# A spatial gating block whose second half is projected with tokens on partitions, and its norm taken along the free axis on VectorE

## The reference

```
z = gelu(x @ w_in_odd)                  # 288 x 1024 times 1024 x 2048
u, v = z[:, :1024], z[:, 1024:]
v = layer_norm(v, sgu_ln_g, sgu_ln_b)   # over the 1024 channels of a token
mix[t, g, c] = sum_s w_s[g, t, s] * v[s, g, c] + b_s[g, t]
                                        # 8 groups g of 128 channels; s <= t in chunks of
                                        # 128 tokens; in each sample over its own 4 tokens
out = (u * mix) @ w_out_odd
x = layer_norm(ALPHA * x + out, ln_g, ln_b)
```

## Time and profile before

| | |
|---|---|
| time, median of 3 runs | 1298.22 us (1296.71 to 1301.53) |
| the profiled execution: time | 1299.01 us |
| its span | 1297.3 us |
| mean granted TensorE clock | 0.952 |
| busy: TensorE | 1195.8 us (92%) |
| busy: VectorE | 493.1 us (38%) |
| busy: ScalarE | 264.3 us (20%) |
| busy: GpSimd | 143.1 us (11%) |
| DMA | 359.97 MB, 277 GB/s over the span |
| the gating block | from about 749 us to about 849 us |

### The profile page before, as it was taken

The page is one execution under the profiler, slowest core; times in us unless marked ns, Lnnn a source line. Parts: engine busy times, 40 slices in busy tenths (PEclk is TensorE's granted clock), DMA queues, the critical chain, the costliest instruction groups (busy, mean ns, idle before and its releaser), DMA issues.

```text
span 1297.3 us, 27118 instructions
## 1 busy us (share of the span) xinstructions
PE 1195.8 (92%) x10881; PEld 780.1 (60%) x10882; DVE 493.1 (38%) x1297; ACT 264.3 (20%) x553; POOL 143.1 (11%) x236
## 2 busy tenths in 40 slices
PE   9999877899997989999998899899998989999996
PEld 7677655566774765555554577676775744555543
DVE  0014561924152362333333500524242553343357
ACT  0013642121141040111111211302230311111113
POOL 2001897000000000000000200000000000000020
PEclk9999889899998979999998999789999889999999
DMA  9746678963378488998999943213367689999994
GB/s 327 260 137 186 206 220 298 389 235 130 130 260 322 146 330 332 383 428 367 429 424 411 382 173 130 69 65 130 130 226 294 228 358 425 427 364 407 417 376 149
DMA packets 89052, 359.97 MB, mean 277 GB/s; under 512 B 7063, under 2 KB 7079, under 8 KB 72586
## 3 DMA queue, kind: packets, MB, share of 16 engines
q1 hardware_dynamic: 81042, 333.73, 67.4%
q0 software_dynamic: 7792, 24.93, 5.3%
q10 hardware_dynamic: 144, 0.27, 0.1%
HBM read 341.48 MB, written 17.85 MB: 277 GB/s over the span
## 4 chain that ended last, share of the span: by engine, by line
PE 69%; DMA 12%; DVE 11%; issue 4%; ACT 3%; SPq 1%; DVEq 0%; POOLq 0%; POOL 0%; ACTq 0%
PE acc L793 37%; PE psS L793 15%; DMA by_slot<-arena 9%; PE psV L793 5%; DVE acts L1603 3%; PE psN L793 2%; PE acc L1142 2%; DVE arena L2015 2%; DMA ring<-in_w_exp_up 2%; PE acc L923 1%; PE psN L1243 1%; PE acc L1273 1%; DMA arena<-by_slot,arena 1%; ACT arena L1482 1%; DMA arena<-in_mem_prompt 1%
## 5 line engine op out<-in xcount | busy, mean ns | idle before, releaser
L793 PE MATMUL acc<-acts,ring 128*128 128x288 f32 x1280 | 319.2, 413 | 3.4 <-DVE acts L1893 1.5
L793 PEld LDWEIGHTS acc<-acts,ring 128*128 128x128 f32 x1280 | 247.1, 193 | 74.5 <-issue 2.5
L793 PE MATMUL psS<-arena,acts 128*32 128x256 f32 (+1 forms) x2864 | 224.2, 390 | 3.0 <-issue 1.7
L793 PEld LDWEIGHTS psS<-arena,acts 128*32 128x32 f32 (+1 forms) x2864 | 98.5, 110 | 82.7 <-issue 42.8
L2015 DVE COPY arena<-psV 32x256 f32<-32x256 f32 x192 | 80.6, 420 | 176.0 <-DMA by_slot<-arena 164.2
L1482 ACT ACTIVATE arena<-acc 128x1024 f32<-128x1024 f32 (+6 forms) x86 | 67.5, 810 | 110.3 <-PE acc L793 35.2
L793 PE MATMUL psS<-ring,acts 128*32 128x256 f32 x1344 | 81.9, 394 | 6.9 <-DMA ring<-in_w_exp_up 3.3
L793 PE MATMUL psS<-acts 128*32 128x256 f32 x672 | 79.4, 386 | 1.6 <-issue 1.6
L2535 POOL DMA_DIRECT2D by_slot<-arena x48 | 23.6, 491 | 447.9 <-DVE arena L2015 447.9
L793 PEld LDWEIGHTS psS<-ring,acts 128*32 128x32 f32 x1344 | 43.9, 113 | 43.3 <-issue 16.3
L2379 ACT ACTIVATE acts<-psS 128x256 f32<-128x256 f32 x54 | 20.7, 383 | 219.8 <-PE psS L793 216.1
(11 more groups left out here) (396 smaller groups left out, 1357.3 us busy)
## 6 DMA issues: line engine op xcount, KB each, us to landing
ring<-in_w_exp_gate SPq DMA_DIRECT2D x17, 2048.0 KB, 13.5
ring<-in_w_exp_up SPq DMA_DIRECT2D x17, 2048.0 KB, 17.0
ring<-in_w_exp_down SPq DMA_DIRECT2D x17, 2048.0 KB, 12.0
acts<-in_w_exp_down SPq DMA_DIRECT2D x10, 2048.0 KB, 17.8
arena<-in_w_exp_gate SPq DMA_DIRECT2D x10, 2048.0 KB, 9.9
arena<-in_w_exp_up SPq DMA_DIRECT2D x10, 2048.0 KB, 16.4
ring<-in_cache_k SPq DMA_DIRECT2D x64, 256.0 KB, 3.2
ring<-in_cache_v SPq DMA_DIRECT2D x64, 256.0 KB, 3.1
```

What stands on the lines that cost most here:

```text
L793: return pe.matmul(out, lhsT, rhs, start=first, stop=last)
```

## The change

The second half of the projection is turned round. The tokens (`xT`) become the stationary operand and the weights stream, 512 columns at a time, so that v lands with tokens on partitions (`token_tile`). The four tiles of the 256 prompt tokens take 8 matmuls of 512 columns each; the 32 sample tokens take 32 matmuls of 256 columns, in four strips of 32 columns of the array. The order is `VT`: rows 0 left half, rows 1 left half, rows 0 right half, samples, rows 1 right half; the turning of the spatial matrices stands before the last.

ScalarE takes Gelu of each tile straight into `gvtok`. VectorE takes the statistics along the free axis (`v_stats`), combines them and adds epsilon (`v_norm`), ScalarE takes the root (`v_root`), and VectorE makes two passes over 1024 columns of each row tile: minus mean times gain, then times reciprocal plus shift. Gain and shift are no longer per-partition columns: GpSimd loads them as rows copied to all partitions (`V_GAIN`, `V_SHIFT`), ahead of its other three loads. The means and variances by TensorE, the scaling and shifting with channels on partitions, and the turning of v with its copies are gone. `WARM_V` is 10 and stands before the mixing. `o1` waits for `mixed` tile by tile. The slots of the last two `in_odd` units are released by other tiles.

Apart from that, `y_rows` of the last norm takes its first pass before the reciprocal, and there ScalarE squares a copy in the on-chip memory in place of the PSUM tile. The helpers `add_squares` and `var_of` lose a branch that only the old norm used.

```diff
@@ -53,7 +53,7 @@
-WARM, WARM_V = 32, 22
+WARM, WARM_V = 32, 10
...
@@ -197,12 +197,10 @@
-add("vv", 8, "s")
-add("vmean", 1, "v")
-add("vvar", 1, "v")
+add("vt", 4, "s")
+t.append(("vt", 4, "s"))
-add("vtok", 6, "vs")
...
@@ -241,6 +239,7 @@
+VT = [(0, 0), (1, 0), (0, 1), (2, 0), (1, 1)]
...
@@ -400,7 +399,7 @@
-        vT = view(0, 8, NTOK)
+        V_GAIN, V_SHIFT = view(0, 1024), view(1024, 1024)
...
@@ -653,7 +650,7 @@
-READER["in_odd", n] = (("u", "vv")[n // 2], 4 * (n % 2) + 3)
+READER["in_odd", n] = ("u", 4 * n + 3) if n < 2 else ("vt", n + 1)
...
@@ -1417,51 +1406,58 @@
     if l:
         for n in range(2):
             project("u", UIDX["in_odd", n], xT, 4 * n, lambda k: evacuated(pe, f"xf{l - 1}", k))
-        for n in range(2):
-            project("vv", UIDX["in_odd", 2 + n], xT, 4 * n)
-        mean_of("vmean", "vv", vT)
-        for _ in range(WARM_V):
-            mm(psN[:, 0:64], ones_d[:, :], ones_d[:, 0:64], True, True)
-        var_of("vvar", "vv", sq_v, 4)
+        Wv = [slot(UIDX["in_odd", 2 + n]).rearrange("p (k n) -> p k n", k=8) for n in range(2)]
+        def token_tile(n):
+            t, half = VT[n]
+            bank_free(pe, "vt", n)
+            for k in range(8):
+                if t < 2:
+                    last = mm(ACC("vt", n), xT[:, k, P * t:P * t + P], Wv[half][:, k, :], k == 0, k == 7)
+                else:
+                    for q in range(4):
+                        last = mm(ACC("vt", n)[32 * q:32 * q + 32, 0:256], xT[:, k, S0:NTOK],
+                                  Wv[q // 2][:, k, 256 * (q % 2):256 * (q % 2) + 256], k == 0, k == 7)
+            last.then_inc(acc_full, 1)
+        arrived(pe, UIDX["in_odd", 2])
+        token_tile(0)
+        token_tile(1)
+        arrived(pe, UIDX["in_odd", 3])
+        token_tile(2)
+        token_tile(3)
         pe.wait_ge(w_masked, 1)
         for i in range(2):
             bank_free(pe, "wm", i)
             for g in range(4):
                 last = pe.transpose(ACC("wm", i)[:, P * g:P * g + P], WLD[:, 4 * i + g, :], ident)
             last.then_inc(acc_full, 1)
+        token_tile(4)
         pe.wait_ge(w_masked, 2)
         bank_free(pe, "wbd", 0)
         for g in range(8):
             last = mm(ACC("wbd", 0)[0:32, 32 * g:32 * g + 32], W4R[:, g].rearrange("p b t -> p (b t)"),
                       cst[0:DS, C_REP:C_REP + 32], True, True)
         last.then_inc(acc_full, 1)
-        for i in range(6):
-            t, half = i // 2, i % 2
-            n = P if t < 2 else 32
-            bank_free(pe, "vtok", i)
-            for f in range(4):
-                if i < 2:
-                    pe.wait_ge(vn_ready, 4 * half + f + 1)
-                last = pe.transpose(ACC("vtok", i)[0:n, P * f:P * f + P],
-                                    vT[:, 4 * half + f, P * t:P * t + n], ident)
-            last.then_inc(acc_full, 1)
-        for i in range(6):
-            evacuated(pe, "vtok", i)
-        evacuated(pe, "wm", 1), evacuated(pe, "wbd", 0)
+        for _ in range(WARM_V):
+            mm(psN[:, 0:64], ones_d[:, :], ones_d[:, 0:64], True, True)
+        evacuated(pe, "wm", 1)
+        pe.wait_ge(v_done, 3)
         for g in range(8):
             bank_free(pe, "mix", g)
             for t in range(2):
                 mm(ACC("mix", g)[:, P * t:P * t + P], gvtok[:, t, P * g:P * g + P], WMT[:, g, :], True, True)
+            evacuated(pe, "wbd", 0)
             mm(ACC("mix", g)[:, S0:NTOK], gvtok[0:32, 2, P * g:P * g + P], WBD[:, g, :], True, True)\
                 .then_inc(acc_full, 1)
-    if l:
-        pe.wait_ge(mixed, 8)
-    else:
+    if l == 0:
         for i in range(4):
             evacuated(pe, "po", i)
     if l:
         for n in range(2):
-            project(f"o{l}", UIDX["out", l, n], mixT, 4 * n)
+            project(f"o{l}", UIDX["out", l, n], mixT, 4 * n, lambda k: pe.wait_ge(mixed, k + 1))
     else:
         for n in range(2):
             project(f"o{l}", UIDX["out", l, n], mixT, 4 * n,
...
@@ -1811,22 +1804,40 @@
 for l in range(DEPTH):
     if l:
-        for i in range(1, 7):
-            evacuated(dve, "vv", i - 1)
-            add_tile("vv", vT, i)
-        evacuated(dve, "vv", 7)
-        center("vmean", vT, 8, cen_v, 2)
-        add_squares("vv", sq_v, 0)
-        rstd("vvar", std_v, 1)
-        for f in range(8):
-            dve.scalar_tensor_tensor(out=vT[:, f, :], in0=vT[:, f, :], scalar=parT[:, f, 12:13],
-                                     in1=rs[:, :], op0=ALU.mult, op1=ALU.mult).then_inc(scl_v, 1)
+        def v_stats(n):
+            t, half = VT[n]
+            r = rows_of[t]
+            evacuated(dve, "vt", n)
+            for h in ((half,) if t < 2 else (0, 1)):
+                ins = dve.bn_stats(STATS[0:r, t, h, :], gvtok[0:r, t, 512 * h:512 * h + 512])
+            link(ins)
+        def v_norm(t, nth):
+            r = rows_of[t]
+            link(dve.bn_aggr(MV[0:r, t, :], STATS[0:r, t].rearrange("p a b -> p (a b)")))
+            dve.tensor_scalar(VE[0:r, t:t + 1], MV[0:r, t, 1:2], EPS, None, ALU.add).then_inc(v_var, 1)
+            dve.wait_ge(v_rows, 32)
+            link(dve.scalar_tensor_tensor(out=gvtok[0:r, t, :], in0=gvtok[0:r, t, :], scalar=MV[0:r, t, 0:1],
+                                          in1=V_GAIN[0:r, :], op0=ALU.subtract, op1=ALU.mult))
+            dve.wait_ge(v_sd, nth)
+            link(dve.reciprocal(RS[0:r, t:t + 1], SD[0:r, t:t + 1]))
+            dve.scalar_tensor_tensor(out=gvtok[0:r, t, :], in0=gvtok[0:r, t, :], scalar=RS[0:r, t:t + 1],
+                                     in1=V_SHIFT[0:r, :], op0=ALU.mult, op1=ALU.add).then_inc(v_done, 1)
+        v_stats(0)
+        v_stats(1)
+        v_stats(2)
+        v_norm(0, 1)
+        v_stats(3)
+        v_norm(2, 2)
         evac(dve, "v", "wm", 2, lambda i, a: dve.tensor_copy(
             WMT[:, 4 * i:4 * i + 4, :], a.rearrange("p (g t) -> p g t", g=4)))
+        v_stats(4)
+        v_norm(1, 3)
         evac(dve, "v", "wbd", 1, lambda i, a: dve.tensor_tensor(
             WBD, a[0:32, 0:256].rearrange("p (g t) -> p g t", g=8),
             cst[0:32, C_BLOCK:C_BLOCK + 32].unsqueeze(1).to_broadcast([32, 8, 32]), ALU.mult))
-        cm["vtok"]()
         for i in range(8):
             evacuated(dve, "u", i)
         for g in range(8):
...
@@ -2103,11 +2114,13 @@
     def y_rows(t, middle, away):
         r = rows_of[t]
-        dve.wait_ge(sd_ready, 3 * l + t + 1)
-        link(dve.reciprocal(RS[0:r, t:t + 1], SD[0:r, t:t + 1]))
+        if t:
+            dve.wait_ge(act_step, 3 * t - 1)
         dve.wait_ge(ln_rows, 32)
         link(dve.scalar_tensor_tensor(out=ROWS_A[0:r, t, :], in0=Z_ROWS[t][0:r], scalar=middle,
                                       in1=GAMMA[0:r, :], op0=away, op1=ALU.mult))
+        dve.wait_ge(sd_ready, 3 * l + t + 1)
+        link(dve.reciprocal(RS[0:r, t:t + 1], SD[0:r, t:t + 1]))
         dve.scalar_tensor_tensor(out=ROWS_A[0:r, t, :], in0=ROWS_A[0:r, t, :], scalar=RS[0:r, t:t + 1],
                                  in1=BETA[0:r, :], op0=ALU.mult, op1=ALU.add).then_inc(y_done, 1)
...
@@ -2307,20 +2320,22 @@
         for i in range(8):
             full(act, "u", i)
             act.activation(qT[:, i, :], ACC("u", i)[:, 0:NTOK], ACT.Gelu).then_inc(emptied["s"], 1)
-        for i in range(8):
-            full(act, "vv", i)
-            act.activation(vT[:, i, :], ACC("vv", i)[:, 0:NTOK], ACT.Gelu).then_inc(emptied["s"], 1)
-        for c in range(4):
-            if c < 3:
-                act.wait_ge(cen_v, c + 1)
+        def v_root(t, nth):
+            r = rows_of[t]
+            act.wait_ge(v_var, nth)
+            act.activation(SD[0:r, t:t + 1], VE[0:r, t:t + 1], ACT.Sqrt).then_inc(v_sd, 1)
+        for n, (t, half) in enumerate(VT):
+            full(act, "vt", n)
+            if t < 2:
+                act.activation(gvtok[:, t, 512 * half:512 * half + 512], ACC("vt", n), ACT.Gelu).then_inc(emptied["s"], 1)
             else:
-                evacuated(act, "vmean", 0)
-            act.activation(mixT[:, 2 * c:2 * c + 2, :], vT[:, 2 * c:2 * c + 2, :], ACT.Square).then_inc(sq_v, 1)
-        root(std_v, "vvar")
-        for f in range(8):
-            act.wait_ge(scl_v, f + 1)
-            act.activation(vT[:, f, :], vT[:, f, :], ACT.Identity, bias=parT[:, f, 13:14]).then_inc(vn_ready, 1)
-        cm["vtok"]()
+                for q in range(4):
+                    ins = act.activation(gvtok[0:32, t, 256 * q:256 * q + 256], ACC("vt", n)[32 * q:32 * q + 32, 0:256],
+                                         ACT.Gelu)
+                ins.then_inc(emptied["s"], 1)
+            if n >= 2:
+                v_root(t, n - 1)
     squares(3 * l)
     memory_values(l, (2,))
     root(std_ready, f"var{3 * l}")
...
@@ -2441,7 +2456,7 @@
-            act.activation(used, z, ACT.Square, bias=middle, accum_out=power).then_inc(act_step, 1)
+            act.activation(used, used, ACT.Square, bias=middle, accum_out=power).then_inc(act_step, 1)
...
@@ -2503,7 +2518,7 @@
```

(43 more changed lines are left out.)

1 line of the change is left out of this document (removed).

## The result

The changed kernel takes 1379.88 us (median of 4 runs, 1376.55 to 1386.86) against 1298.45 us before: ratio 1.0631, 95% interval 1.0585 to 1.0678. Slower by 81 us, where 26 us less were forecast. The profiled execution took 1386.86 us, span 1385.1.

A forecast was written before the change was run, and what follows sets the result against it. TensorE, busy 92% of the span, was taken to bound the kernel through its waits and slow stretches. Gains of 25.8 us (gating block) and 0.3 (end) made 26.1, forecast 1272.5 us; range 1270 to 1276, 8 in 10 1269.5 to 1283.

The forecast's parts named there:

- Nothing is late behind it: Gating block: removing the old norm's work delays nothing after it; its time is already counted in the 14.8 us.
- so they move with it: Layer 1's expert loads: they waited for TensorE, 106.1 us in 8 waits, so they start earlier along with it.
- The prediction's own sign: Test: prediction is wrong if mixing starts after 822 or the distance from `o1`'s first residual to kernel end grows.
- rival 2: Layer 1's experts: the gain is given back to load waits; no change, 1298, or in part 1276 to 1280; chance 0.05.
- rival 3: Norm's first VectorE pass: gain rows load late, delaying the mixing; slower, 1309 if they land at 841; chance 0.01.
- I take the clock to stay at 2.4 GHz: Mixing and `o1`'s start: TensorE keeps full clock through a 1.6 us gap; 0.86 us a mixing group, not 1.72.
- rival 1: Mixing: the clock falls all the same, mixing takes 13.8 us, kernel 1282.5; chance 0.20 with midway forms.
- the two clock terms: Gains from full clock: 6.9 us in the mixing and 3.1 us in `o1`'s first tile.
- the schedule of the norm: Between projection and mixing: the norm's steps end at 818.9, so mixing starts at 819.0, 14.8 us sooner.
- 4: Sample tile's matmuls: the strips do not run side by side, 11 us more, 1283.5; chance 0.04 including small losses.
- The gain of the block: Gating block through `o1`'s first tile: ends at 829.8 instead of 855.6, a gain of 25.8 us.
- The end: Last norm: VectorE's passes follow on and end at 1294.65 instead of 1294.96, a gain of 0.3 us.

The follow-up runs named there:

- experiment 6: Kernel before with 97 already-met wait instructions added on TensorE ahead of layer 1's expert loop: 1303.01 us, ratio 1.0074.
- experiment 8: Kernel before with 107 already-met wait instructions added on TensorE ahead of layer 1's expert loop: 1324.4 us, ratio 1.0131.
- experiment 10: Kernel before with 157 already-met waits ahead of layer 0 and 99 more ahead of layer 1's loop: median 1320.25 us over 8 executions.
- 2: Kernel before with 127 already-met wait instructions added on TensorE ahead of layer 1's expert loop: 1400.03 us, ratio 1.0776.
- 7: Kernel before with 153 already-met wait instructions added on TensorE ahead of layer 1's expert loop: 1400.83 us, ratio 1.079.
- 4: Kernel before with 64 already-met wait instructions added on TensorE ahead of layer 1's expert loop: 1302.04 us, ratio 1.003.
- dense kernel: Changed kernel with 4 dense 512-column matmuls replacing the 10 small ones ahead of the mixing, plus 64 already-met waits: 1276.99 us, ratio 0.9869.
- experiment 9: Changed kernel with 127 already-met wait instructions added behind layer 1's expert loop, at the end of TensorE's program: 1380.01 us, ratio 1.062.
- experiment 1: Changed kernel with 127 already-met wait instructions on TensorE, putting layer 1's expert loop back where it was: 1284.36 us, ratio 0.9901.

## Why the prediction was wrong

- **The step that failed**: of what is removed, "Nothing is late behind it", and of the expert loads, "so they move with it". Removed instructions were priced by their time alone. They have a place too, and everything behind them in TensorE's program moves: the loop landed where it is fetched in every pass. Price: 100.4 us in layer 1's experts, against 26.1 forecast in all. The prediction's own sign showed it: from the first residual to the end 441.7 us became 544.3. No rival had it; rival 2 looked at the right stretch for the wrong cause (the load queue), and the sign of rival 3 for another. Rows 1 to 11 could not have shown it, since the kernel before was fast, but its code has the long loop and its page the queue of instruction packets, and a chance for that belonged in the range.
- **The clock.** "I take the clock to stay at 2.4 GHz" failed; rival 1 was right. Granted clock 0.50 from about 821, 13.75 us of mixing (rival 1: 13.8), and 1284.36 and 1283.46 with the loop repaired (rival 1: 1282.5). The gap was 1.61 us (forecast 1.6). That the gap was the reason is likely, not shown: the clock fell in five of five profiled executions with it, and in neither of the two with the wait filled. In the kernel before the low clock is no fixed cost either: its mixing took 7.84 us in the profiled executions of experiments 6, 8 and 10, 12.3 in those of 2 and 7, 13.75 in that of 4 and 13.76 in the earlier trace rows. So the 10 us of the two clock terms (6.9 for the mixing, 3.1 for the first tile of `o1`) were there to be won in some executions only.
- **Right: the schedule of the norm.** The mixing started 15.24 us sooner relative to u (forecast 14.8), with Gelu of 128x512 at 0.60 and the table loads at 1.28. No drain: in the rows above the loads at 806.52 and 808.04 have the root between them, and the activation at 809.53 follows the second load by 0.2 us, so the further drain of some 1380 ns of the Trainium skill's "ScalarE: Activation LUTs", section "What ACT_TABLE_LOAD costs", did not appear. Rivals 3 and 4 did not happen: VectorE's first pass with the gain rows (at 807.65) had no wait for them, and the 64 instructions of the strips took 3.6 us (805.80 to 809.39).
- **The gain of the block: right against one execution, too high in general.** With the clock kept it is 25.1 us against 25.8, but measured from an execution of the kernel before whose mixing ran at the low clock throughout. Where the mixing of before took 7.84 us, Gelu to residual took 64.48 (experiment 6), 65.97 (8) and 64.21 us (10), and the dense kernel's 48.60 are 15.6 to 17.4 less. The medians lie between: the dense kernel is 18.1 us faster than the kernel before beside it (1295.12), where 26.1 were forecast. What was counted too high is the clock, 10 us of the 25.8; the terms of the norm's schedule held.
- **The end.** From the end of its last `z_stats` to its last pass the dense kernel took 8.1 us, before 8.76: 0.65 won, forecast 0.3. The passes follow on a little more closely than the 1.31 us of the sum: three of them start 0.08 us before the instruction ahead has ended.
- **Missed: 2.25 us between the first residual and the router.** Forecast as nothing. The router's sums ran partly at the low clock. Stages of the kernel before, then of the dense kernel, at that place:

```profile
1025.00:1028.00 3.00, 3.00 (x38) 2.94 (x37) 2.21 (x6) 2.95 (x5) 0.00 (x0) 1.00 0.72 303
```

```profile
999.00:1001.00 2.00, 2.00 (x17) 2.00 (x16) 1.79 (x3) 1.98 (x5) 0.00 (x0) 0.79 1.02 434
1001.00:1003.00 2.00, 2.00 (x22) 1.93 (x22) 0.65 (x4) 1.20 (x1) 0.00 (x0) 0.50 0.13 53
```

  From the first residual to the router's last group of products the profiled executions of the change take 176.0 to 176.5 us, but 172.4 in experiment 9. Those of the kernel before take 174.1 to 174.2, but 176.8 in experiment 8 and 176.9 in experiment 10. So both kernels have it in some executions, and it cannot be put down to the change. Why the clock falls earlier there was not tried.
- **The sum, put right.** For the dense kernel: -1.3 (u ends earlier in this execution) - 25.1 + 2.25 + 0.24 = -23.9 = 1273.4 - 1297.3. Forecast -26.1. This compares two single executions, one with the low clock in the mixing and one without; the medians side by side differ by 18.1 us.

## What to carry to other kernels

An edit that adds or removes instructions ahead of a long loop has a second effect that no account of busy time shows: compare the packets of the instruction queue and the "issue" waits first when a stretch that was not edited gets slower, and try the edit with some do-nothing instructions ahead of the loop before judging it. Place such a loop where it was fast (a shorter loop may help too; that was not tried), since one unlucky position costs more here than the edit could bring. Where TensorE's clock may fall in a wait, filling the wait to its end is worth trying: in the profiled executions the mixing took 6 us less with it, though the medians do not show that gain. And before a low clock is counted as a cost that can be won back, look at several profiled executions of the kernel before: here it was there in some and not in others.

## What the runs showed of the hardware

- A loop of 1598 instructions (100 KB at 64 bytes each) on TensorE is run five times from one fetch at 33, 97, 130, 194, 202, 210 and 226 past a multiple of 256 (52 packets in the whole kernel), is fetched in every pass at 160, 162 and 186 (87 to 89), and once more at 140 (61). The Trainium skill's "Advanced Engine Details and Errata", section "ISA Cache", gives TensorE 128 KB in lines of 16 KB, which agrees with a loop of seven such blocks being kept; its "Only 2 cache lines!", if it is meant for TensorE, does not, as with two lines the loop would be refetched in every pass everywhere. The Trainium skill's "Runtime: NRT & Kernel Launch", section "Instruction fetch mechanics", has fetching "mostly hidden"; in the straight program it is (11 packets from 700 to 1010 us in the kernel before, whose longest "issue" wait anywhere is 2.5 us), in the refetched loop the 9 packets of a pass cost 15 to 27 us. The bad stretch is over 46 and under 64 positions long, which agrees with the 61 at which a loop of this length touches an eighth block, but it does not begin where the plain count has it. Why the bad positions are these and not others stays open.
- The slow position costs twice: TensorE idles 68.7 us more in that stretch, and is busy 31.7 us longer with the same 3501 instructions, at a mean granted clock of 0.80 in place of 0.96.
- A wait that is already met costs TensorE 0.1 us: 77 such instructions filled a gap of 8.0 us in experiment 1, and 54 one of 5.5 us in experiment 8.
- Whether TensorE's clock is low in a given stretch differs between executions of one kernel: the mixing of the kernel before, with waits added ahead of it at most, took 7.84 us in three of seven profiled executions, 12.3 in two and 13.75 in two.
